# Decode cross scores head by head beneath the cross query panels, prompt head 0 with them, and four banks for the cross output tiles

## Chip, core and metric

The kernel runs on one core of one Trainium2 chip. The metric is the device time of one execution in microseconds. The engines are called PE (TensorE), DVE (VectorE), ACT (ScalarE), POOL (GpSimd) and SP (SyncE) as in the profile; each runs its own instructions in order and waits on semaphores.

## What is computed

One inference step of a one-layer decoder trunk for 256 prompt tokens and 8 decode users of one token each (264 token columns in all), width 2048. The part that matters here is the cross attention over 256 memory tokens, with 4 heads of 128:

```
def cross_attn(h, mk, mv, w_q, w_o):
    q = (h @ w_q).reshape(B, T, X_HEADS, X_HEAD_DIM)
    s = jnp.einsum('bthd,bmhd->bhtm', q, mk, preferred_element_type=jnp.float32) * (X_HEAD_DIM ** -0.5)
    p = jax.nn.softmax(s, axis=-1).astype(mv.dtype)
    o = jnp.einsum('bhtm,bmhd->bthd', p, mv).reshape(B, T, X_DIM)
    return o @ w_o
```

h is the normalised residual. All prompt tokens share one memory, whose keys and values the kernel computes itself (tile mkv). Each decode user b has its own cached memory keys and values. Before this stands the mixer with its output projection, behind it a SwiGLU of 5632 and a final norm. Everything is fp32.

## The kernel before

**Weight panels.** A projection is a list of panels of 2048x128 weights (1 MB). SP loads a panel into one of four raw slots. ACT rounds it to whi (L565, `cast`), DVE forms wlo = raw - whi (L993, `split`), and PE makes three matmuls for each of 16 blocks (L1554 to L1556, `three`): whi by hh, whi by hl, wlo by hh, all 264 columns wide, into one of banks 0 and 1. So a panel has 48 matmuls. DVE evicts the bank. The handshakes are the semaphores w_hi, w_split, mm_done and acc0_free / acc1_free. In `step`, ACT waits for the end of panel k before it casts panel k+2; DVE waits for the end of panel k, evicts its tile and then splits panel k+2. The order of the lists is: in, mem, out, xq, xo, gu0, dn0, gu1, dn1.

**xq** is the cross query projection: four panels, panel k giving head k of x_q (feature by token: 128 x 264; columns 256 to 263, called DEC, are the decode users). In its first panel PE also sums the squares of the norm (L1606, L1608); ACT takes the root (L579, with a table load), DVE the reciprocal (L1019), and `to_q` (L1385) multiplies each evicted tile by it.

**The block between xq and xo** has two interleaved parts, whose order is written out by hand on each engine.
Decode scores, user by user: DVE spreads x_q's column of user b on diagonals (`x_diag`, L1392, 128x512), PE multiplies it by ones so that every partition has the query of all four heads (`x_spread`, L1886, banks 2 and 3), ACT copies it scaled to x_qb (`x_query`, L858), and DVE makes eight products with sum (`x_scores`, L1401): two halves of the memory by four heads, keys in page (partition = memory token), each 128x128. The keys of all eight users have been loaded long before; the last product for user b releases POOL's fetch of the values of user b into the same page slot (`fetch`, L466). Then softmax over the memory for all 32 (user, head) pairs: maximum (L1453, transpose L1946, L1456, L1457, L1948), subtraction (L1462), Exp (L922), sums (L1467, L1952), reciprocal (L1469). `x_pv` (L1896) multiplies by the values per user, ACT takes the result (`x_take`, L864), `x_extract` (L1902) picks the diagonal.
Prompt heads 0 to 3: `x_stage` (ACT: a_q L869, a_v L870, a_vn L872), `x_head` (PE: transposes L1909, scores L1912), `x_max` (DVE: L1412 to L1414), `x_exp` (ACT, L878), `x_rec` (DVE), `x_scale` (ACT, L886), `x_turned` (PE, L1921), `x_pt` (ACT, L892), `x_out` (PE, L1928, L1929), `x_out_hi` (ACT, L896) and `x_out_lo` (DVE, L1423). Even heads use banks 6 and 7 and one set of buffers, odd heads banks 0 and 1 and another. In the block the order is heads 0 and 1 with the decode scores, then heads 2 and 3 with the rest.

**xo** is the cross output: four panels, each of which makes four output tiles of 12 matmuls (contraction over 4 heads), 16 tiles c = 4k + j in all, in banks 0 and 1 in turn. It starts when DVE has finished all of the block (xo_go). DVE adds each tile to the residual x_res (L1490), ACT makes the next norm's hh (`norm_hi`, L583) and the square (L591), which POOL adds up (L484), and DVE makes hl one tile later (`norm_lo`, L1014). The split of panel k+2 stands behind tile 3 of panel k. **gu0** follows, whose first panel waits block by block for hl and again contains the sum of squares.

## Time and profile before

| | us |
|---|---|
| median of 3 runs | 1657.13 (1654.46 to 1662.43) |
| the profiled execution, its own time | 1656.92 |
| its span | 1655.2 |
| PE busy, share | 1519.4, 92% |
| DVE, ACT, POOL busy | 1034.0, 617.6, 229.0 |
| mean granted clock of PE | 0.967 |

The span runs from the first to the last recorded instruction; what lies around it is the difference to the execution's own time. A granted clock of 1.0 is 2.4 GHz, of 0.5 it is 1.2 GHz; a value between them is a mean over a stretch. "Idle before" in a row is how long the engine stood still ahead of the instruction, and the name behind it is what ended that.

### The profile page before, as it was taken

How to read it: one execution, taken by the hardware profiler on the slowest of the kernel's cores; microseconds unless marked ns; L12 is line 12 of the kernel's file. 1: busy time of each engine (PE TensorE's matmuls, PEld its weight loads, DVE VectorE, ACT ScalarE, POOL GpSimd, SP SyncE). 2: the span in 40 equal slices, each digit the busy share in tenths (PEclk: the TensorE clock that was granted, in tenths of full speed). 3: DMA queues.
4: the chain of work that ended last, by engine and by line, in shares of the span. 5: the costliest groups of instructions: out<-in, count | busy, mean ns of one | idle time of the engine just before them, and what ended most of it. 6: DMA issues, size and time to landing. Idle time of an engine off the chain costs nothing.

```text
span 1655.2 us, 32624 instructions
## 1 busy us (share of the span) xinstructions
PE 1519.4 (92%) x12197; PEld 1399.3 (85%) x12197; DVE 1034.0 (62%) x3234; ACT 617.6 (37%) x725; POOL 229.0 (14%) x331
## 2 busy tenths in 40 slices
PE   4999987899998898996779999999999999999997
PEld 4999854577776677995579999999999999999996
DVE  4579899898977876656455555553445555554444
ACT  3343233232143553443344333333333333333443
POOL 3011222222222222330120000000000000000221
PEclk9999989899998999998789999999999999999998
DMA  8558999999998899453225555544555555553553
GB/s 318 178 186 304 402 365 404 404 372 375 379 387 295 294 377 402 167 179 120 77 102 178 177 180 184 185 163 146 185 175 204 180 180 184 186 182 123 183 182 122
DMA packets 78979, 388.42 MB, mean 235 GB/s; under 512 B 9096, under 2 KB 9872, under 8 KB 56864
## 3 DMA queue, kind: packets, MB, share of 16 engines
q1 hardware_dynamic: 35424, 230.90, 39.1%
q0 software_dynamic: 39376, 143.15, 23.1%
q10 hardware_dynamic: 4080, 13.12, 2.0%
q8 instruction: 53, 0.87, 0.2%
q14 instruction: 46, 0.38, 0.1%
HBM read 377.03 MB, written 10.10 MB: 234 GB/s over the span
## 4 chain that ended last, share of the span: by engine, by line
PE 75%; DVE 13%; DMA 5%; ACT 4%; issue 3%; POOLq 0%; ACTq 0%; DVEq 0%; SPq 0%; POOL 0%
PE bank L1554 23%; PE bank L1555 22%; PE bank L1556 22%; DVE page L1084 4%; DVE wlo L1028 2%; DMA page<-kc_dram 2%; PE bank L1711 2%; DMA page<-vc_dram 1%; DVE wlo L993 1%; ACT whi L602 1%; DMA raw<-p_out_dram 1%; ACT whi L565 1%; DMA raw<-p_in_dram 1%; DVE rstd L1019 1%; PE bank L1886 1%
## 5 line engine op out<-in xcount | busy, mean ns | idle before, releaser
L1554 PE MATMUL bank<-hh,whi 128*128 128x264 f32 (+1 forms) x2368 | 693.5, 293 | 36.2 <-DVE wlo L1028 23.5
L1555 PE MATMUL bank<-hl,whi 128*128 128x264 f32 (+1 forms) x2368 | 677.4, 286 | 0.0
L1556 PE MATMUL bank<-hh,wlo 128*128 128x264 f32 (+1 forms) x2368 | 677.1, 286 | 0.0
L993 DVE TENSOR_TENSOR wlo<-raw,whi 128x2048 fp32r<-128x2048 f32 (+1 forms) x174 | 356.2, 2047 | 281.4 <-ACT whi L565 281.4
L1554 PEld LDWEIGHTS bank<-hh,whi 128*128 128x128 f32 x2368 | 452.7, 191 | 72.9 <-issue 38.7
L565 ACT ACTIVATE whi<-raw 128x2048 fp32r<-128x2048 f32 (+1 forms) x174 | 299.3, 1720 | 545.0 <-PE bank L1556 537.6
L1555 PEld LDWEIGHTS bank<-hl,whi 128*128 128x128 f32 x2368 | 453.2, 191 | 0.5 <-issue 0.2
L1556 PEld LDWEIGHTS bank<-hh,wlo 128*128 128x128 f32 x2368 | 450.7, 190 | 0.0
L1084 DVE CUSTOM_DVE_ANT_0 page<-page,qb 128x128 f32<-128x128 f32 x1024 | 226.4, 284 | 18.3 <-ACT qb L647 11.3
L1554 PE MATMUL bank<-f_hi,whi 128*128 128x264 f32 x704 | 202.2, 287 | 7.5 <-DVE f_lo L1526 7.5
L1556 PE MATMUL bank<-f_hi,wlo 128*128 128x264 f32 x704 | 201.5, 286 | 0.0
L1555 PE MATMUL bank<-f_lo,whi 128*128 128x264 f32 x704 | 200.3, 285 | 0.0
L484 POOL TENSOR_TENSOR s_acc<-s_acc,s_sq 128x264 f32<-128x264 f32 x45 | 71.4, 1588 | 826.6 <-ACT s_sq L591 826.0
L602 ACT ACTIVATE whi<-raw 128x2048 fp32r<-128x2048 f32 x58 | 110.9, 1911 | 163.2 <-PE bank L1556 150.9
L1028 DVE TENSOR_TENSOR wlo<-raw,whi 128x2048 fp32r<-128x2048 f32 x58 | 138.1, 2380 | 40.9 <-ACT whi L602 40.8
L1554 PEld LDWEIGHTS bank<-f_hi,whi 128*128 128x128 f32 x704 | 134.0, 190 | 7.9 <-issue 7.9
L1555 PEld LDWEIGHTS bank<-f_lo,whi 128*128 128x128 f32 x704 | 134.2, 191 | 0.0
L1556 PEld LDWEIGHTS bank<-f_hi,wlo 128*128 128x128 f32 x704 | 134.0, 190 | 0.0
L466 POOL DMA_DIRECT2D page<-kc_dram x128 | 67.6, 529 | 323.0 <-DVE s_raw L1084 293.6
L1711 PE MATMUL bank<-page,prob 128*8 128x256 f32 x1024 | 80.6, 393 | 25.7 <-DMA page<-vc_dram 13.0
L466 POOL DMA_DIRECT2D page<-vc_dram x128 | 67.6, 528 | 147.7 <-PE bank L1711 89.5
L1084 DVE DVE_READ_ACCUMULATOR2_ANT s_raw<- 128x1 f32 x1024 | 82.1, 80 | 0.0
(295 smaller groups left out, 1441.9 us busy)
## 6 DMA issues: line engine op xcount, KB each, us to landing
raw<-p_gu_dram SPq DMA_DIRECT2D x88, 1024.0 KB, 4.9
page<-kc_dram POOLq DMA_DIRECT2D x128, 512.0 KB, 8.6
page<-vc_dram POOLq DMA_DIRECT2D x128, 512.0 KB, 9.1
raw<-p_in_dram SPq DMA_DIRECT2D x48, 1024.0 KB, 8.3
raw<-p_dn_dram SPq DMA_DIRECT2D x64, 704.0 KB, 4.1
raw<-p_out_dram SPq DMA_DIRECT2D x16, 1024.0 KB, 5.5
raw<-p_mem_dram SPq DMA_DIRECT2D x8, 1024.0 KB, 8.3
x_res<-x_fm_dram SPq DMA_DIRECT2D x8, 528.0 KB, 10.3
```

The costliest lines, as they stand in the source:

```text
L466: pool.dma_start(dst, src).then_inc(S(f"page_in{slot}"), 16)
L484: pch.link(pool.tensor_tensor(s_acc[:, :], s_acc[:, :], s_sq[:, c % 2, :], ALU.add))
L565: act.activation(whi[:, kk % 2, 0:blocks * P], raw[:, kk, 0:blocks * P], ACT.Copy).then_inc(S("w_hi"), 1)
L602: act.activation(whi[:, p % 2, :], raw[:, ring(p) % 4, :], ACT.Copy).then_inc(S("w_hi"), 1)
L993: tt(wlo[:, (k + 2) % 4, 0:blocks * P], raw[:, (k + 2) % 4, 0:blocks * P], whi[:, k % 2, 0:blocks * P], ALU.subtract).then_inc(S("w_split" ...
L1019: ch.link(dve.reciprocal(rstd[:, 0:n], rstd[:, 0:n]))
L1028: tt(wlo[:, k, :], raw[:, k, :], whi[:, p % 2, :], ALU.subtract).then_inc(S("w_split"), 1)
L1084: ins = dve.tensor_tensor_reduce(out=pk, in0=pk, in1=qb[:, P * h:P * h + P], scale=1.0, scalar=0.0, op0=ALU.mult, op1=ALU.add, accum_out=s ...
L1554: mm(out, blk(whi, k % 2, b), rh, start=start, stop=False)
L1555: mm(out, blk(whi, k % 2, b), rl, start=False, stop=False)
L1556: return mm(out, blk(wlo, k, b), rh, start=False, stop=stop)
L1711: last = mm(bank[4][32 * g:32 * g + H, 0:256], prob[:, u % 2, v, :], page[:, slot, 256 * g:256 * g + 256], start=v == 0, stop=v == PAGES - 1)
```

## The change

- The decode scores go head by head. When head h of x_q is there, PE transposes its eight decode columns to rows (`x_rows`, 8x128, bank 5), ACT copies them scaled to x_qr, and PE spreads each user's row over the partitions with a matmul of contraction 8 (one column of the identity, broadcast), eight of them, 128 columns each, into banks 2 and 3. DVE's products read the query straight from these banks. x_qd and x_qb are gone.
- PE's four xq panels are cut into quarters of four blocks. Between them stand, for panel k, the rows and the spread of head k-1; and prompt head 0: `x_head(0)` in panel 1, `x_turned` in panel 2, `x_out` in panel 3. ACT and DVE get the same order. So three heads of scores and prompt head 0 lie beneath the xq panels, the fourth head of scores and prompt heads 1 to 3 behind them.
- The fetch of a user's values is released by the score of the last head.
- xo's tile j of each panel goes to bank j, so that four tiles can be open. ACT casts the next panel ahead of norm_hi of tile 3, and DVE splits it after tile 0 of the next panel.
- Five semaphores of the softmax become two counted ones.

The diff, with the indentation cut by up to twelve blanks:

```diff
@@ -314,8 +314,7 @@
 x_q = view(at("x_q", C0 + 32 * TW, [P, XH, T]), XH, T)
-x_qd = at("x_qd", C0 + 4 * TW, [P, 512])
-x_qb = view(at("x_qb", C0 + 6 * TW, [P, 2, 512]), 2, 512)
+x_qr = at("x_qr", C0 + 4 * TW, [ND, XH * P])
 x_s = view(at("x_s", C0 + 10 * TW, [P, ND, 2, XH]), ND, 2, XH)
@@ -847,15 +846,10 @@
         step("out", i, k, C)
-step("xq", 0, 0, C)
-norm_root(2, T)
-for k in range(1, 4):
-    step("xq", 0, k, C)
-def x_query(b):
-    act.wait_ge(S("xq_ps"), b + 1)
-    if b >= 2:
-        act.wait_ge(S("xk_used"), b - 1)
-    act.activation(x_qb[:, b % 2, :], bank[2 + b % 2][:, :], ACT.Copy, scale=SCALE).then_inc(S("xq_b"), 1)
+def x_rows(k):
+    act.wait_ge(S("xq_ps"), k + 1)
+    act.activation(x_qr[:, P * k:P * k + P], bank[5][0:ND, 256:384], ACT.Copy, scale=SCALE).then_inc(S("xq_rows"), 1)
@@ -866,6 +860,7 @@
     wait_apart(act, "a_free", i + 1)
+    act.wait_ge(S(f"acc{i % 2}_free"), ACC["xq"] // 2 + i // 2 + 2)
     act.activation(a_q[:, :], x_q[:, i, 0:NP_], ACT.Copy, scale=SCALE)
@@ -895,52 +890,55 @@
+step("xq", 0, 0, C)
+norm_root(2, T)
+x_rows(0)
 x_stage(0)
+step("xq", 0, 1, C)
+x_exp(H)
+x_rows(1)
+x_scale(H)
+step("xq", 0, 2, C)
+x_pt(H)
+x_rows(2)
+step("xq", 0, 3, C)
+x_out_hi(H, 0)
+x_rows(3)
 x_stage(1)
-x_query(0)
-x_query(1)
-x_exp(H)
+x_stage(2)
 x_exp(H + 1)
-x_query(2)
-x_query(3)
-x_scale(H)
+x_exp(H + 2)
 x_scale(H + 1)
-x_pt(H)
 x_pt(H + 1)
-x_query(4)
-x_query(5)
-x_out_hi(H, 0)
-x_query(6)
-x_query(7)
-x_out_hi(H + 1, 1)
-x_stage(2)
-x_stage(3)
-x_exp(H + 2)
-x_exp(H + 3)
+x_scale(H + 2)
 act.wait_ge(S("x_sub"), 1)
 act.activation(x_p[:, :, :, 0:XH], x_s, ACT.Exp).then_inc(S("x_exp"), 1)
-x_scale(H + 2)
-x_scale(H + 3)
 x_pt(H + 2)
-x_pt(H + 3)
+x_out_hi(H + 1, 1)
 x_take(0)
+x_stage(3)
+x_exp(H + 3)
 x_take(1)
...
 x_take(2)
+x_scale(H + 3)
 x_take(3)
+x_pt(H + 3)
+x_take(4)
+x_take(5)
 x_out_hi(H + 3, 3)
-for b in range(4, ND):
-    x_take(b)
+x_take(6)
+x_take(7)
 act.wait_ge(S("xod_ready"), 1)
...
         c = 4 * k + j
+        if j == 3:
+            step("xo", 0, k, C)
         act.wait_ge(S(f"acc{j % 2}_free"), ACC["xo"] // 2 + c // 2 + 2)
...
         square(3, c, x_res[:, c:c + 1, :])
-    step("xo", 0, k, C)
@@ -1383,24 +1381,20 @@
     tt(x_q[:, k, :], bank[k % 2][:, 0:T], rstd[:, :], ALU.mult).then_inc(S(f"acc{k % 2}_free"), 1)
-panels("xq", to_q)
-ch.link(dve.memset(x_p, 0.0))
-def x_diag(b):
-    if b:
-        dve.wait_ge(S("xq_ps"), b)
-    tt(x_qd[:, :].rearrange("p (a b) -> p a b", a=XH), row(ident).broadcast_to([P, XH, P]),
-       x_q[:, :, NP_ + b:NP_ + b + 1].broadcast_to([P, XH, P]), ALU.mult).then_inc(S("xq_diag"), 1)
-def x_scores(b):
-    dve.wait_ge(S("xq_b"), b + 1)
-    dve.wait_ge(S(f"page_in{b}"), 16 * 33)
-    for m in range(2):
-        for h in range(XH):
+def x_scores(h):
+    dve.wait_ge(S("xq_spread"), h + 1)
+    for b in range(ND):
+        if h == 0:
+            dve.wait_ge(S(f"page_in{b}"), 16 * 33)
+        for m in range(2):
             pk = page[:, b, 512 * m + P * h:512 * m + P * h + P]
-            ins = dve.tensor_tensor_reduce(out=pk, in0=pk, in1=x_qb[:, b % 2, P * h:P * h + P], scale=1.0, scalar=0.0,
-                                           op0=ALU.mult, op1=ALU.add, accum_out=x_s[:, b, m, h:h + 1])
-    ins.then_inc(S("xk_used"), 1)
+            ins = dve.tensor_tensor_reduce(out=pk, in0=pk, in1=bank[2 + b // 4][:, P * (b % 4):P * (b % 4) + P], scale=1.0,
+                                           scalar=0.0, op0=ALU.mult, op1=ALU.add, accum_out=x_s[:, b, m, h:h + 1])
+        if h == XH - 1:
+            ins.then_inc(S("xk_used"), 1)
+    if h < XH - 1:
+        ins.then_inc(S("x_scored"), 1)
@@ -1424,50 +1418,43 @@
 x_start()
-x_diag(0)
+ch.link(dve.memset(x_p, 0.0))
+step("xq", 0, 0, C, to_q)
+x_scores(0)
 x_max(H)
-x_diag(1)
+step("xq", 0, 1, C, to_q)
+x_rec(H)
+x_scores(1)
+step("xq", 0, 2, C, to_q)
+x_scores(2)
+step("xq", 0, 3, C, to_q)
+x_out_lo(H, 0)
+x_start()
 x_max(H + 1)
-x_scores(0)
-x_diag(2)
-x_scores(1)
-x_diag(3)
-x_rec(H)
-x_rec(H + 1)
-x_scores(2)
-x_diag(4)
 x_scores(3)
-x_diag(5)
-x_scores(4)
-x_diag(6)
-x_scores(5)
-x_diag(7)
-x_out_lo(H, 0)
-x_scores(6)
-x_scores(7)
-x_out_lo(H + 1, 1)
-x_start()
-x_start()
 own("xk_used", ND)
 bh = "p (b h) -> p b h"
-tt(x_sm[:, 0:32].rearrange(bh, b=ND), x_s[:, :, 0, :], x_s[:, :, 1, :], ALU.max).then_inc(S("xmx_ready"), 1)
+tt(x_sm[:, 0:32].rearrange(bh, b=ND), x_s[:, :, 0, :], x_s[:, :, 1, :], ALU.max).then_inc(S("x_small"), 1)
+x_rec(H + 1)
 x_max(H + 2)
-dve.wait_ge(S("xmx_ps"), 1)
+dve.wait_ge(S("x_small_ps"), 1)
 ch.link(dve.tensor_reduce(x_sm[0:32, 64:65], bank[5][0:32, 0:P], AX.X, ALU.max))
-ts(x_sm[0:32, 96:128], ident[0:32, 0:32], x_sm[0:32, 64:65], None, ALU.mult).then_inc(S("xm_diag"), 1)
-x_max(H + 3)
-dve.wait_ge(S("xm_ps"), 1)
+ts(x_sm[0:32, 96:128], ident[0:32, 0:32], x_sm[0:32, 64:65], None, ALU.mult).then_inc(S("x_small"), 1)
+x_rec(H + 2)
+dve.wait_ge(S("x_small_ps"), 2)
 mb = bank[5][:, P:P + 32].rearrange(bh, b=ND)
...
 ins.then_inc(S("x_sub"), 1)
-x_rec(H + 2)
+dve.wait_ge(S("x_exp"), 1)
+tt(x_sm[:, 32:64].rearrange(bh, b=ND), x_p[:, :, 0, 0:XH], x_p[:, :, 1, 0:XH], ALU.add).then_inc(S("x_small"), 1)
+x_out_lo(H + 1, 1)
+x_start()
+dve.wait_ge(S("x_small_ps"), 3)
+dve.reciprocal(x_sm[:, 128:160], bank[5][:, 160:192]).then_inc(S("x_small"), 1)
+own("x_small", 4)
+x_max(H + 3)
 x_rec(H + 3)
-dve.wait_ge(S("x_exp"), 1)
-tt(x_sm[:, 32:64].rearrange(bh, b=ND), x_p[:, :, 0, 0:XH], x_p[:, :, 1, 0:XH], ALU.add).then_inc(S("xl_part"), 1)
-dve.wait_ge(S("xl_ps"), 1)
-dve.reciprocal(x_sm[:, 128:160], bank[5][:, 160:192]).then_inc(S("xl_read"), 1)
-own("xl_read", 1)
 x_out_lo(H + 2, 2)
@@ -1487,11 +1474,11 @@
         xs = x_res[:, c, :]
-        tt(xs, bank[j % 2][:, 0:T], xs, ALU.add).then_inc(S(f"acc{j % 2}_free"), 1)
+        tt(xs, bank[j][:, 0:T], xs, ALU.add).then_inc(S(f"acc{j % 2}_free"), 1)
         if c:
             norm_lo(3, c - 1, 3, x_res[:, c - 1, :], hh, hl, T)
-    if k < 3:
-        split(first, 0, k + 2, C)
+        if k and j == 0:
+            split(first, 0, k + 1, C)
 norm_lo(3, C - 1, 3, x_res[:, C - 1, :], hh, hl, T)
@@ -1877,13 +1864,36 @@
     out_panel(c)
-four_panels("xq")
-def x_spread(b):
-    pe.wait_ge(S("xq_diag"), b + 1)
-    if b >= 2:
-        pe.wait_ge(S("xq_b"), b - 1)
-    mm(bank[2 + b % 2][:, :], ones, x_qd[:, :], start=True, stop=True).then_inc(S("xq_ps"), 1)
+def x_quarter(k, q):
+    if q == 0:
+        pe.wait_ge(S("w_split"), ST["xq"][0] + k + 1)
+        pe.wait_ge(S(f"acc{k % 2}_free"), ACC["xq"] // 2 + k // 2 + 1)
+    for b in range(4 * q, 4 * q + 4):
+        if k == 0:
+            if b == C - 1:
+                norm_sum(2)
+            pe.wait_ge(S("n_lo_done"), 2 * C + b + 1)
+        last = three(bank[k % 2][:, 0:T], (k + 2) % 4, b, hh[:, b, 0:T], hl[:, b, 0:T], b == 0, b == C - 1)
+    if q == 3:
+        last.then_inc(S("mm_done"), 1)
+def x_rows(h):
+    pe.wait_ge(S(f"acc{h % 2}_free"), ACC["xq"] // 2 + h // 2 + 2)
+    if h:
+        pe.wait_ge(S("xq_rows"), h)
+    pe.transpose(bank[5][0:ND, 256:384], x_q[:, h, DEC], ident).then_inc(S("xq_ps"), 1)
+def x_spread(h):
+    pe.wait_ge(S("xq_rows"), h + 1)
+    if h:
+        pe.wait_ge(S("x_scored"), h)
+    for b in range(ND):
+        last = mm(bank[2 + b // 4][:, P * (b % 4):P * (b % 4) + P], ident[0:ND, b:b + 1].broadcast_to([ND, P]),
+                  x_qr[:, P * h:P * h + P], start=True, stop=True)
+    last.then_inc(S("xq_spread"), 1)
@@ -1928,38 +1938,52 @@
-x_head(0)
+for k in range(4):
+    x_quarter(k, 0)
+    if k:
+        x_rows(k - 1)
+    x_quarter(k, 1)
+    if k:
+        x_spread(k - 1)
+    x_quarter(k, 2)
+    if k == 1:
+        x_head(0)
+    elif k == 2:
+        x_turned(H)
+    elif k == 3:
+        x_out(H)
+    x_quarter(k, 3)
+x_rows(3)
+for k in range(2):
+    pe.wait_ge(S(f"acc{k}_free"), ACC["xq"] // 2 + 3)
 x_head(1)
-for b in range(4):
-    x_spread(b)
-x_turned(H)
+x_spread(3)
+x_head(2)
+pe.wait_ge(S("x_small"), 1)
+pe.transpose(bank[5][0:32, 0:P], x_sm[:, 0:32], ident).then_inc(S("x_small_ps"), 1)
 x_turned(H + 1)
-x_spread(4)
-x_spread(5)
-x_out(H)
-x_spread(6)
-x_spread(7)
+pe.wait_ge(S("x_small"), 2)
+mm(bank[5][:, P:P + 32], ones[0:32, :], x_sm[0:32, 96:128], start=True, stop=True).then_inc(S("x_small_ps"), 1)
+x_turned(H + 2)
 x_out(H + 1)
-x_head(2)
+pe.wait_ge(S("x_small"), 3)
+mm(bank[5][:, 160:192], ones, x_sm[:, 32:64], start=True, stop=True).then_inc(S("x_small_ps"), 1)
+x_pv(0)
 x_head(3)
-pe.wait_ge(S("xmx_ready"), 1)
-pe.transpose(bank[5][0:32, 0:P], x_sm[:, 0:32], ident).then_inc(S("xmx_ps"), 1)
-pe.wait_ge(S("xm_diag"), 1)
-mm(bank[5][:, P:P + 32], ones[0:32, :], x_sm[0:32, 96:128], start=True, stop=True).then_inc(S("xm_ps"), 1)
-x_turned(H + 2)
-x_turned(H + 3)
-pe.wait_ge(S("xl_part"), 1)
-mm(bank[5][:, 160:192], ones, x_sm[:, 32:64], start=True, stop=True).then_inc(S("xl_ps"), 1)
-x_pv(0)
 x_pv(1)
 x_out(H + 2)
-pe.wait_ge(S("xl_read"), 1)
+pe.wait_ge(S("x_small"), 4)
 x_extract(0)
...
 x_pv(3)
+x_turned(H + 3)
+x_extract(2)
+x_pv(4)
+x_extract(3)
+x_pv(5)
 x_out(H + 3)
-for b in range(4, ND + 2):
+for b in range(6, ND + 2):
     x_extract(b - 2)
@@ -1967,9 +1991,9 @@
     for j in range(4):
-        pe.wait_ge(S(f"acc{j % 2}_free"), ACC["xo"] // 2 + 2 * k + j // 2 + 1)
+        pe.wait_ge(S(f"acc{j % 2}_free"), ACC["xo"] // 2 + 2 * k + j // 2)
         for b in range(XH):
-            last = three(bank[j % 2][:, 0:T], (k + 2) % 4, XH * j + b, oh[:, b, :], ol[:, b, :], b == 0, b == XH - 1)
+            last = three(bank[j][:, 0:T], (k + 2) % 4, XH * j + b, oh[:, b, :], ol[:, b, :], b == 0, b == XH - 1)
         last.then_inc(S("xo_tile" if j < 3 else "mm_done"), 1)
```

## Rows read from the trace of the kernel before

**Rows 1.** The page, parts 1 and 2: busy time; and GB/s moved in 40 slices
```profile
PE 1519.4 (92%) x12197; PEld 1399.3 (85%) x12197; DVE 1034.0 (62%) x3234; ACT 617.6 (37%) x725; POOL 229.0 (14%) x331
...
GB/s 318 178 186 304 402 365 404 404 372 375 379 387 295 294 377 402 167 179 120 77 102 178 177 180 184 185 163 146 185 175 204 180 180 184 186 182 123 183 182 122
```

**Rows 2.** Windows of core 0: us, PE, PEld, DVE, ACT, POOL busy, PEclk, DMA share, GB/s
```profile
742.60:764.30 21.70, 19.15 (x144) 18.80 (x143) 9.70 (x7) 7.51 (x5) 0.00 (x0) 0.92 0.43 146
764.30:776.00 11.70, 5.72 (x15) 3.84 (x14) 5.65 (x8) 4.21 (x8) 0.00 (x0) 0.71 0.26 90
776.00:801.10 25.10, 15.19 (x30) 6.70 (x30) 20.52 (x142) 11.46 (x26) 5.25 (x8) 0.73 0.40 130
801.10:823.90 22.80, 17.31 (x177) 13.37 (x177) 5.91 (x19) 10.34 (x32) 0.43 (x1) 0.78 0.12 43
...
830.50:868.00 37.50, 28.63 (x191) 27.87 (x190) 19.61 (x30) 17.73 (x30) 9.39 (x13) 0.86 0.32 113
sum 125.40, PE 92.59 PEld 77.17 DVE 64.32 ACT 53.75 POOL 17.44; mean PE 15.43 PEld 12.86 DVE 10.72 ACT 8.96 POOL 2.91
```

**Rows 3.** The timeline beneath the xq panels: start us, us, engine, line, what, idle before
```profile
742.61 1.92 ACT L565 ACTIVATE whi<-raw 128x2048 fp32r<-128x2048 f32 x1 [3.51 <-PE bank L1556]
...
748.26 0.43 DVE L1385 TENSOR_TENSOR x_q<-bank,rstd 128x264 f32<-128x264 f32 x1
748.43 1.91 ACT L565 ACTIVATE whi<-raw 128x2048 fp32r<-128x2048 f32 x1 [2.11 <-PE bank L1556]
...
750.95 0.44 PE L1554 MATMUL bank<-hh,whi 128*128 128x264 f32 x1 [2.55 <-DVE wlo L993]
...
753.17 0.42 PE L1555 MATMUL bank<-hl,whi 128*128 128x264 f32 x1
...
753.39 0.42 PE L1556 MATMUL bank<-hh,wlo 128*128 128x264 f32 x1
...
764.41 1.91 ACT L565 ACTIVATE whi<-raw 128x2048 fp32r<-128x2048 f32 x1 [3.89 <-PE bank L1556]
```

**Rows 4.** Groups of the block, 764.3 to 823.9 us: count, busy us, mean ns, idle before
```profile
L1401 DVE CUSTOM_DVE_ANT_0 page<-page,x_qb 128x128 f32<-128x128 f32 x64 | 14.1, 287 | 0.0
L1886 PE MATMUL bank<-x_qd,kst 128*128 128x512 f32 x16 | 12.4, 867 | 6.3 <-DVE x_qd L1392 6.3
...
L1392 DVE TENSOR_TENSOR x_qd<-kst,x_q 128x512 f32<-128x512 f32 x8 | 5.5, 690 | 6.1 <-PE bank L1886 5.9 <-DVE x_p L1387 0.2
L1401 DVE DVE_READ_ACCUMULATOR2_ANT x_s<- 128x1 f32 x64 | 5.3, 82 | 0.0
L858 ACT ACTIVATE x_qb<-bank 128x512 f32<-128x512 f32 x8 | 4.8, 594 | 12.1 <-PE bank L1886 12.1
```

**Rows 5.** The timeline within the block
```profile
778.33 1.28 ACT L878 ACT_TABLE_LOAD   x1
...
803.93 1.92 PE L1912 MATMUL bank<-mkv,a_q 128*128 128x256 f32 x4
...
810.19 1.97 PE L1921 MATMUL bank<-kst,a_s 128*128 128x128 f32 x8 [3.18 <-ACT a_s L886]
...
813.51 0.28 ACT L864 ACTIVATE x_o<-bank 128x128 f32<-128x128 f32 x1 [0.71 <-PE bank L1896]
```

**Rows 6.** A group of VectorE over the whole span: a 128x128 copy out of a bank
```profile
L1235 DVE COPY t_s<-bank 128x128 f32<-128x128 f32 x8 | 2.2, 275 | 0.0
```

**Rows 7.** The timeline of ScalarE and VectorE in the xo panels
```profile
826.15 0.52 ACT L583 ACTIVATE hh<-x_res,gains 128x264 fp32r<-128x264 f32 x1 [2.57 <-DVE x_res L1490]
...
831.22 1.90 ACT L565 ACTIVATE whi<-raw 128x2048 fp32r<-128x2048 f32 x1
...
833.15 2.29 DVE L993 TENSOR_TENSOR wlo<-raw,whi 128x2048 fp32r<-128x2048 f32 x1 [2.16 <-ACT whi L565]
835.36 0.42 DVE L1490 TENSOR_TENSOR x_res<-bank,x_res 128x264 f32<-128x264 f32 x1
```

**Rows 8.** The instructions that fetch decode values: ns min/median/max, first and last start
```profile
L466 POOL DMA_DIRECT2D page<-cmv_dram x8: 709/710/713, 780.1 to 800.8; - x8
```

## The prediction

> **What bounds it now.** The page comes first: TensorE (PE) is busy 92% of the span [rows 1], so a change pays only where PE stands still or runs at its low clock. The table of windows comes next, because the share hides the stages: in the 125.4 us from 742.6 to 868.0 PE is busy 92.6, and its granted clock is 0.71 to 0.78 in the three stretches that make up the cross attention block [rows 2]. Everything that the change touches lies there. Beneath the xq panels PE waits for VectorE's split of panel 2 [rows 3]. From 764.4 to 823.9, 59.5 us, no weight panel runs: that is the block. In the xo panels PE stops once per panel, because evictions stand behind a split on VectorE [rows 7]. The timeline gives the order within each stretch, the groups the prices.
>
> Durations are those of the profiled execution: 1656.92 us, 1.7 above its span and 0.2 under the median 1657.13. Less than 0.5% from the median (1648.8 to 1665.4) is what a measurement of this kernel can hardly tell from no change.
>
> **Prices.** A panel is 48 matmuls; panel 1 of xq ran from 742.6 to 748.4, 5.8 us, so 0.12 each; at the low clock starts are 0.22 apart [rows 3], so the low clock costs 0.10 a matmul. Cast 1.9, split 2.3, eviction 0.43, norm_hi 0.52 [rows 3, 7]. The 64 score instructions took 14.1 us, 0.22 each, with the accumulator read beneath the next one [rows 4]: one head, 16 of them, is 3.5 us.
>
> **Part A, the xq panels (742.6 to 764.4 before).** They now carry three heads of decode scores and prompt head 0.
> - PE runs quarter 0 of panel 1 (1.45 us, to 744.05) and then waits for the eviction of tile 0, since the row transpose reads x_q. That eviction ends at 748.7, after Sqrt and reciprocal [rows 3]. For 4.65 us three quarters of panel 1 stand behind it in PE's queue. Before, PE worked through this and idled 2.55 us afterwards [rows 3].
> - The mean clock of 0.92 over 21.7 us [rows 2] is 3.5 us at the low level, right after that idle time. I carry the fall over to the new stall: some 20 matmuls at 0.10, 2.1 us.
> - x_spread(h) is 8 fp32 products, K=8, 128 columns, two passes each: no row has that shape. Eight 128-column transposes took 1.97 us at the low clock [rows 5], 0.25 each. Above: 16 x 0.25 = 3.9 us. Below: half of it at full clock, 1.8. I take 1.8 beneath the panels, where PE is hot: three are 5.4.
> - Head 0's V transposes and scores 1.1, four transposes 0.45, output 0.85, each about half of its low-clock row [rows 5]: 2.4. Three row transposes of 0.2: 0.6.
> - ScalarE copies each row (0.28 [rows 5]) in its own order. Walked through: quarter 1 ends at 751.6, spread 753.9, quarter 2 755.3, head 0 756.5, panel 1 757.9. ScalarE then casts to 759.9 and does head 0's Exp with its 1.28 us table load [rows 5]; the copy for head 1 is ready at 762.7, PE arrives at 761.2: 1.5 us. In the other rounds the copy is there first. VectorE's scores(0) and maximum end at 759.0, so eviction 1 and split 3 stand behind them 1.1 us, which PE, in quarter 0 of panel 2 until 759.4, hardly feels; scores(1) and (2) end before their evictions are due.
> - Sum from 742.6: panels 17.4, stall 4.65, clock 2.1, spreads 5.4, head 2.4, rows 0.6, copy 1.5 = 34.0, to 776.6. **A = +12.2 us.**
>
> SP loads the same panels, one after each finished panel; panels are now 9 us apart, so the loads hide. The x_p memset moves beneath VectorE's wait for Sqrt.
>
> **Part B, the block (59.5 us before).** Gone are eight diagonals (5.5 us), eight spreads through ones (16 passes, 12.4 busy and 6.3 idle) and eight copies of 512 columns (4.8, with 12.1 idle before them) [rows 4]. They formed a ring: diagonal, spread, copy, eight scores. After the panels only the last head's scores are left. From 776.6: cast 1.9, head 0's output copy 0.4, row copy 0.3, staging of head 1 0.8, with hand-offs 3.5; head 1's V transposes and scores at the low clock 2.1 (1.92 for the four passes [rows 5]); spread(3) between 1.8 and 3.9, I take 2.6; 16 scores 3.5. That is 11.7: decode scores are done at 788.3, before at 801.1.
> The tail from there (maximum over keys, Exp, sums, values, extraction, two prompt heads) took 22.8 us [rows 2]. It now also holds the rest of head 1: transposes 0.9 and output 1.7 at the low clock, 25.4. xo starts at 813.7. **B = 37.1 - 59.5 = -22.4 us.**
> POOL's eight fetches of decode values went out one per user between 780.1 and 800.8 [rows 8]; now the last head releases all eight between about 785 and 788. At 0.71 us each on POOL the last issue is near 791.5; 4.2 MB at the 404 GB/s of the page's best slices [rows 1] take 10.4 us, so the last lands by about 802 and the first values product at 797, the last at 810, find theirs. I cost them at nothing; if that cover fails, 3 us.
>
> **The operand in PSUM.** The scores now take their second input from a bank. A 128x128 copy from a bank takes 275 ns, the score instruction from SBUF 287 [rows 6, 4]: no surcharge shows, and I take none. Bounds: nothing, to an exposed accumulator read of 0.08 on each, 1.3 us a head.
> The Trainium skill says the contrary (VectorE: DVE Perf Modes, The TRN2 errata): a fixed 120 cycles from PSUM against 58 from SBUF, and its Rules for kernel authors advise a copy to SBUF where many operations follow. An estimate from that page is 65 ns more each, 4.1 us over 64; with half of it on the path the sum would be 1638.
>
> **Part C, xo to the end of gu0's first panel (823.9 to 868.3, 44.4 us).** Before, VectorE made the split for panel k+2 right after tile 3 of panel k, with cast 831.2, split 833.2 to 835.4 and only then an eviction [rows 7], while two banks let PE go two tiles on: a period of 10.6 us for 5.8 of work. Now four banks carry PE across the border, the cast starts before norm_hi of tile 3, and the split follows tile 0 of the next panel. From xo's start T: PE ends panel 0 at T+5.8; cast to 7.8, norm_hi(3) and norm_lo(3) to 8.9, split to 11.2, before PE needs it at 11.6. Then ScalarE, with four norm_hi and squares a panel, falls behind: cast to 15.3, split 16.3 to 18.6, PE stalls 1.2; cast to 22.7, split to 26.0, PE, done at 24.4, stalls 1.6. gu0's first panel with its norm sum takes 6.7: T+32.7. For bursts on ScalarE and POOL I add 1: T+33.7. **C = -10.7 us.**
>
> **Sum:** 12.2 - 22.4 - 10.7 = -20.9; 1656.9 - 20.9 = 1636.0.
>
> **The rivals.**
> - **Small costs add up** (15%). Spreads at 3.9 (+2.1 three times, +1.3) and slower scores, 3 us of it on the path: +10.6, 1646.6. For it: K=8 products and copies of eight rows have no row. Against: the transposes' rows.
> - **xo keeps half its stalls** (10%), since norm_lo(c-1) waits for ScalarE, which now casts first: 2.4 us more in three panels, 1643.
> - **Slower: the low clock rules** (5%). Quarters now end in small products that wait on other engines, and 2.55 us of idle time were followed by the low clock [rows 3]. Place and price: xq panels 1 to 3 (144 matmuls) and xo with gu0's first panel (240) at 0.10 each, 38 us, less the 2 charged, plus 4 in the block: +40, 1676. It decides from 20.9 / 0.10, some 210 of those 384 matmuls. Against: beneath the panels and in xo I find no gap over 1.6 us but the one of 4.65.
> The Trainium skill knows such a case (TensorE: Matmul & The Clock Gate, A second HAM failure mode): a kernel that cycled through PSUM banks with short idle times had its clock alternate.
> - **More overlaps** (12%). Head 1 hides in the tail (-2.6), spread(3) at full clock (-0.8), no fall in panel 1 (-2.1), xo without its lag (-2.5): 1628.
> - **The change buys nothing** (3%). Scores 1 and 2 hold the evictions and PE waits each time: what leaves the block stands in the panels. Each hold would need 10 us; a head's scores are 3.5.
>
> **How the numbers follow.** Forecast 55%, its own range 1630 to 1642. With the rivals next to it 1627 to 1650 holds 8 in 10. Faster by over 0.5%: forecast, more overlap, xo's rival and most of the small costs, less what I overlooked: 0.82. Within 0.5%: 0.12. Slower: 0.06.
>
> **What would show it.** A: the last xq panel ends near 776.6, PE waits once for 4.7 us on x_q, and head 0's Exp stands beneath the panels. B: the last decode score is near 788, xo's first matmul near 813.7, and no values product waits for a transfer. C: gu0's first panel ends 33.7 us after xo's start, with PE waits of under 3 us in it. Score instructions stay at 0.22 us. I am wrong if the xq panels end after 782, if the clock from 742 to 868 is under 0.8, or if xo's period stays over 8 us.

## The result, and the profile after

The median went from 1659.94 us (1654.46 to 1663.26, 7 runs) to 1648.53 us (1647.55 to 1649.99, 7 runs): ratio 0.9934, 95% interval 0.9919 to 0.9949. That is 11.4 us less; forecast were 20.9. The profiled execution took 1649.72 us with a span of 1648.0, 1.2 over its median, and the one of the kernel before lies 3.0 under its median. So this pair of traces (1656.92 and 1649.72) differs by 7.2 us only, and the stretches below are held against those 7.2.

Three stretches can be cut at the same marks in every trace: the xq panels after the first, the block, and xo with gu0's first panel. The marks are ScalarE's casts at the ends of xq's first and last panel and of gu0's first, and xo's first product.

| us | before | forecast | after | after less forecast |
|---|---|---|---|---|
| xq panel 0 to panel 3 | 21.8 | 34.0 | 43.6 | +9.6 |
| block | 59.5 | 37.1 | 36.1 | -1.0 |
| xo to the end of gu0's first panel | 44.5 | 33.7 | 38.35 | +4.65 |

The table of windows of the kernel after, first the three gaps between xq's panel ends, then block and tail, then xo (us, then PE, PEld, DVE, ACT, POOL busy, PEclk, DMA share, GB/s):

```profile
743.10:762.90 19.80, 15.05 (x74) 14.01 (x73) 9.42 (x39) 4.96 (x8) 0.00 (x0) 0.66 0.15 53
762.90:776.10 13.20, 11.65 (x71) 11.19 (x70) 6.29 (x35) 5.33 (x9) 0.00 (x0) 0.74 0.23 81
776.10:786.70 10.60, 10.60 (x70) 9.75 (x68) 6.14 (x34) 2.54 (x3) 0.00 (x0) 0.84 0.28 100
786.70:799.30 12.60, 8.68 (x30) 6.56 (x29) 7.96 (x38) 5.41 (x13) 2.55 (x4) 0.59 0.32 104
799.30:822.90 23.60, 16.20 (x180) 12.30 (x180) 6.72 (x23) 10.64 (x33) 3.20 (x6) 0.79 0.45 168
822.90:830.50 7.60, 7.60 (x50) 7.60 (x51) 2.24 (x5) 2.49 (x6) 1.86 (x4) 0.78 0.01 2
830.50:861.20 30.70, 26.30 (x198) 25.64 (x198) 22.29 (x31) 17.34 (x30) 16.27 (x14) 0.94 0.41 137
```

The clock beneath xq's panels was 0.92 [rows 2]; now it is 0.66, 0.74, 0.84. The last xq panel has no wait at all (10.60 busy of 10.60) and still takes 10.6 us, where the prediction's prices give 8.65 (5.8 for the panel, 1.8 for the spread, 0.85 for head 0's output, 0.2 for the row). TensorE's timeline beneath these panels shows the waits and the spreads:

```profile
749.31 0.38 PE L1886 MATMUL bank<-kst,x_q 128*8 128x128 f32 x1 [4.75 <-DVE x_q L1383]
752.25 3.78 PE L1894 MATMUL bank<-x_qr,kst 8*128 8x128 f32 x16
767.41 2.87 PE L1894 MATMUL bank<-x_qr,kst 8*128 8x128 f32 x16 [1.55 <-ACT x_qr L852]
779.06 2.04 PE L1894 MATMUL bank<-x_qr,kst 8*128 8x128 f32 x16
782.00 0.34 PE L1542 MATMUL bank<-hl,whi 128*128 128x264 f32 x1
782.13 0.42 PE L1543 MATMUL bank<-hh,wlo 128*128 128x264 f32 x1
782.36 0.42 PE L1541 MATMUL bank<-hh,whi 128*128 128x264 f32 x1
```

Both waits are the forecast ones, 4.75 for 4.65 and 1.55 for 1.5. But the clock falls three times, not once. It is at 0.50 from about 748 to 761.6, a fall that comes within the wait of 4.75 us and ahead of the first spread; from 768.5 to 775.3, a fall within the second spread, behind the wait of 1.55; and from 782.1 to 785.5. The last rows show this third one: inside panel matmuls, with nothing idle before them, 1 us after a spread, the starts go from 0.13 to 0.23 us apart. Of 135 recorded panel matmuls of the three panels, some 51 start 0.22 us after the one before, the others 0.12 after it.

The groups of the score instructions and of POOL's fetches, from 742 to 800 us, and the whole fetch on POOL's timeline:

```profile
L1392 DVE CUSTOM_DVE_ANT_0 page<-page,bank 128x128 f32<-128x128 f32 x64 | 13.6, 282 | 10.4 <-PE bank L1894 10.4
L1392 DVE DVE_READ_ACCUMULATOR2_ANT x_s<- 128x1 f32 x64 | 5.2, 82 | 0.0
...
796.75 5.74 POOL L465 DMA_DIRECT2D page<-cmv_dram  x8 [61.23 <-DVE x_s L1392]
```

A score instruction takes 282 ns from PSUM where it took 287 from SBUF [rows 4]. The fetches go out in one run at the end, from 796.75 to 802.5, and no values product waits for a transfer: the first starts at 808.76, where the forecast had 797.

The timeline of xo, one period of it:

```profile
830.52 1.92 ACT L564 ACTIVATE whi<-raw 128x2048 fp32r<-128x2048 f32 x1
833.24 0.77 POOL L483 TENSOR_TENSOR s_acc<-s_acc,s_sq 128x264 f32<-128x264 f32 x1 [2.03 <-ACT s_sq L590]
833.29 2.86 DVE L991 TENSOR_TENSOR wlo<-raw,whi 128x2048 fp32r<-128x2048 f32 x1
834.18 2.58 POOL L483 TENSOR_TENSOR s_acc<-s_acc,s_sq 128x264 f32<-128x264 f32 x1 [0.18 <-POOL s_acc L483]
838.17 1.90 ACT L564 ACTIVATE whi<-raw 128x2048 fp32r<-128x2048 f32 x1
...
843.82 0.39 PE L1541 MATMUL bank<-oh,whi 128*128 128x264 f32 x1 [1.55 <-DVE wlo L991]
852.72 0.36 PE L1541 MATMUL bank<-hh,whi 128*128 128x264 f32 x1 [2.85 <-issue]
```

The cast before, one panel after the one at 831.22 [rows 7]:

```profile
841.80 1.90 ACT L565 ACTIVATE whi<-raw 128x2048 fp32r<-128x2048 f32 x1
```

The period is 7.65 us (cast to cast), where it was 10.6, and my walk had 7.5. Two things are new. The split takes 2.86 us where it took 2.3 [rows 7]: it starts 0.05 us after a GpSimd addition of 0.77 us, and the next addition, which starts inside the split, takes 2.58 instead of 0.75 and ends 0.6 us behind it. And PE waits 2.85 us before gu0's first panel, 1.4 us beyond the end of the split that it needs (851.31).

### The profile page after: what moved, and what is told of

The parts are those of the page before. It is cut to its first block, busy times and chain, and to the rows that moved or that the text cites. A ratio compares the mean times of both kernels' runs of the same rounds, so it can differ in the third digit from the quotient of the medians.

```text
span 1648.0 us, 32704 instructions
## 1 busy us (share of the span) xinstructions
PE 1521.5 (92%) x12249; PEld 1408.8 (85%) x12249; DVE 1031.0 (63%) x3226; ACT 612.7 (37%) x721; POOL 235.1 (14%) x331
## 4 chain that ended last, share of the span: by engine, by line
PE 74%; DVE 14%; DMA 5%; ACT 4%; issue 3%; ACTq 0%; DVEq 0%; SPq 0%; POOLq 0%; POOL 0%
PE bank L1541 22%; PE bank L1542 21%; PE bank L1543 21%; DVE page L1082 4%; DVE wlo L1026 3%; DMA page<-kc_dram 2%; PE bank L1698 2%; ACT whi L601 1%; ACT whi L564 1%; DMA raw<-p_out_dram 1%; DVE wlo L991 1%; PE bank L1894 1%; DMA raw<-p_in_dram 1%; DMA page<-vc_dram 1%; DVE rstd L1017 1%
## 5 line engine op out<-in xcount | busy, mean ns | idle before, releaser
L1082 DVE CUSTOM_DVE_ANT_0 page<-page,qb 128x128 f32<-128x128 f32 x1024 | 226.2, 283 | 16.5 <-ACT qb L646 11.4
L483 POOL TENSOR_TENSOR s_acc<-s_acc,s_sq 128x264 f32<-128x264 f32 x45 | 77.5, 1723 | 815.5 <-ACT s_sq L590 814.4
L1698 PE MATMUL bank<-page,prob 128*8 128x256 f32 x1024 | 79.8, 389 | 24.1 <-issue 12.6
```

The lines of the kernel that those rows point to most:

```text
L483: pch.link(pool.tensor_tensor(s_acc[:, :], s_acc[:, :], s_sq[:, c % 2, :], ALU.add))
L1082: ins = dve.tensor_tensor_reduce(out=pk, in0=pk, in1=qb[:, P * h:P * h + P], scale=1.0, scalar=0.0, op0=ALU.mult, op1=ALU.add, accum_out=s ...
L1698: last = mm(bank[4][32 * g:32 * g + H, 0:256], prob[:, u % 2, v, :], page[:, slot, 256 * g:256 * g + 256], start=v == 0, stop=v == PAGES - 1)
```

## Experiments

Theory A: the fp32 products that contract over 8 rows take the clock down. Its rivals: the idle times do it, or the quarters' small pieces. For xo, D: a wait for a bank that is already free; and E: VectorE and GpSimd hold each other up.

**Spreads contracted over 128 rows** (kernel after; x_qr has 120 more rows of zeros, so that the products give the same):

```diff
-x_qr = at("x_qr", C0 + 4 * TW, [ND, XH * P])
+x_qr = at("x_qr", C0 + 4 * TW, [P, XH * P])
...
-last = mm(bank[2 + b // 4][...], ident[0:ND, b:b + 1].broadcast_to([ND, P]),
+last = mm(bank[2 + b // 4][...], ident[:, b:b + 1].broadcast_to([P, P]),
...
+ch.link(dve.memset(x_qr[:, :], 0.0))
```

> The changed kernel with one edit: the spread's products contract over 128 partitions instead of 8 (the rows of x_qr below the eighth are zero), same number of passes, same columns, same result. Theory A (the K=8 products themselves bring the low clock): in the changed kernel the clock is low from 748 to 761.6, 768.9 to 775.3 and 782.5 to 785.2, each around a spread; with K=128 the clock beneath the xq panels returns within 4 us of the 4.75 us stall and does not fall after the spreads of panels 2 and 3. The three xq panels after the first shorten from 43.6 to about 35 us, the time falls by 8 to 10 us, to about 1639. Theory B (only PE's waits bring it: 4.75 us on x_q, 1.55 us on the row copy): nothing changes beyond 1 us, the clock pattern stays, 1648.

1641.22 us (1638.44 to 1643.08), ratio to before 0.9882 (0.9863 to 0.9902), 7.3 us under the kernel after. Its windows from the end of xq panel 0 to that of panel 3:

```profile
746.80:762.90 16.10, 11.35 (x73) 11.03 (x72) 8.40 (x37) 4.94 (x7) 0.00 (x0) 0.79 0.17 65
762.90:772.90 10.00, 8.54 (x72) 8.19 (x71) 7.06 (x38) 5.35 (x9) 0.00 (x0) 1.00 0.30 107
772.90:781.50 8.60, 8.55 (x69) 8.21 (x67) 6.16 (x37) 2.56 (x4) 0.00 (x0) 1.00 0.36 123
```

43.6 us have become 34.7. The idle times and the pieces are all still there (4.75 and 1.46 us of waits), and from 759 us on the clock stays at 1.0 to the end of the panels. Only the fall at the long wait is left, the one that the prediction charged. So the rivals fall for the second and the third fall, and idle time stays the likely cause of the first.

One trace is not enough to price this. The spreads over 8 rows stand unchanged in four other kernels below. The one without xo's part again takes 43.6 us here; the other three take 37.7 to 37.9. All five show the three falls; what differs is the first, which lasts some 13.6 us in two of them and 3.4 in three. The windows of one of the three (the kernel of "Earlier cast and split in xo"):

```profile
748.00:763.70 15.70, 10.94 (x74) 10.27 (x73) 8.64 (x37) 4.98 (x8) 0.00 (x0) 0.89 0.19 67
763.70:775.40 11.70, 10.14 (x71) 9.79 (x70) 6.90 (x38) 5.33 (x10) 0.00 (x0) 0.85 0.27 91
775.40:786.00 10.60, 10.53 (x69) 9.65 (x67) 6.17 (x35) 2.57 (x4) 0.00 (x0) 0.84 0.28 100
```

Against those, the wider contraction takes off 3.8 us in the second and third gap (22.3 to 18.55) and nothing in the first (16.1). The medians are 7.3 us apart, and the runs of the two kernels don't overlap.

**The products by themselves**, in the kernel before, in the dense panels of the mixer's output projection: first one group each of 8 products over 8 and over 128 rows, behind the eighth block of panels 4 and 10, then longer groups in panels 2, 5, 9 and 13.

```diff
+if n == 7 and c in (2, 5, 9, 13):
+    kp, count = {2: (ND, 8), 5: (ND, 16), 9: (ND, 32), 13: (P, 32)}[c]
+    for d in range(count):
+        mm(bank[5][:, P * (d % 4):P * (d % 4) + P], ident[0:kp, d % 8:d % 8 + 1].broadcast_to([kp, P]),
+           x_res[0:kp, 0, 0:P], start=True, stop=True)
```

> The kernel before, with two groups of eight fp32 products of 128 columns (16 passes each, as one spread) put into the middle of two out panels, where PE never waits: contraction 8 in panel 4, contraction 128 in panel 10, same moving operand, into bank 5, where nobody reads them. Nothing of the computation is left out. Theory A: after the K=8 group the matmul starts go from 0.12 to 0.22 us apart for some us, without any idle time before; after the K=128 group they stay 0.12. Theory B: both stay at 0.12 and each group costs its own 1.8 us only.

> The kernel before, with groups of fp32 products of 128 columns inside out panels, where PE never waits, into bank 5, unread; nothing is left out. Panel 2: 8 products of contraction 8 (1.8 us, as one spread); panel 5: 16 (3.6 us); panel 9: 32 (7.1 us); panel 13: 32 of contraction 128. One group of 8 in dense work had left the clock at 1.0. Theory A2 (products of contraction 8 count as rest, so the clock falls when there are enough of them, or when other rest stands beside them): the clock falls in or after the 32 of panel 9, perhaps after the 16 of panel 5, and not after the 32 full ones of panel 13. Theory B (contraction does not matter): it stays 1.0 in all four.

The first (1664.15 us, one execution) did not show the effect: the clock stayed at 1.0 behind both groups. The second (1688.74 us, one execution) shows it, and more of it with more products. Its windows: three around the 16 products over 8 rows, which run from 678.1 to 683.1; three around the 32 over 8 rows, from 708.4 to 719.9; and one at the end of the 32 over 128 rows, which run from 745.4 to 752.7:

```profile
679.00:681.00 2.00, 2.00 (x18) 2.00 (x17) 1.48 (x2) 0.00 (x0) 1.19 (x1) 0.88 0.45 176
683.00:685.00 2.00, 2.00 (x9) 1.89 (x9) 0.00 (x0) 0.00 (x0) 0.00 (x0) 0.50 0.00 0
687.00:689.00 2.00, 2.00 (x17) 2.00 (x17) 0.43 (x1) 0.78 (x1) 0.00 (x0) 0.91 0.00 0
710.00:712.00 2.00, 2.00 (x17) 2.00 (x16) 0.76 (x1) 0.00 (x0) 0.47 (x1) 0.81 0.07 25
718.00:720.00 2.00, 2.00 (x10) 1.77 (x10) 0.00 (x0) 0.00 (x0) 0.00 (x0) 0.50 0.00 0
724.00:726.00 2.00, 2.00 (x15) 2.00 (x15) 0.43 (x1) 0.69 (x1) 0.00 (x0) 0.77 0.00 0
752.00:754.00 2.00, 2.00 (x19) 2.00 (x18) 0.00 (x0) 0.00 (x0) 0.00 (x0) 1.00 0.00 0
```

PE is busy 2.00 of 2.00 us in each, so no idle time comes in. 8 products over 8 rows: no fall. 16: low from 680.5 to 687.3. 32: low from 711.2 to 724.9. 32 over 128 rows: none. Both falls come while the products are still running. So these products themselves bring the low clock when there are enough of them. In the kernel after, a spread is only 8 products, and the clock falls within the second and behind the third, where one group of 8 in dense work did nothing; what else counts there (the wait of 1.55 us, row transposes, the falls before, the head's pieces) stays open.

**The two halves of the change alone.** xo's part in the kernel before, and the kernel after without it:

```diff
+if j == 3:
+    step("xo", 0, k, C)
-tt(xs, bank[j % 2][:, 0:T], xs, ALU.add)
+tt(xs, bank[j][:, 0:T], xs, ALU.add)
-if k < 3:
-    split(first, 0, k + 2, C)
+if k and j == 0:
+    split(first, 0, k + 1, C)
```

> The kernel before with the xo part alone (four banks, cast ahead of norm_hi of tile 3, split after tile 0 of the next panel). If the profile's split of the gain is right, xo to the end of gu0's first panel goes from 44.4 to 38 us and the time falls by 5 to 7 us (ratio about 0.996). Rival, my blind forecast: 33.7 us in that stretch and 10.7 us less, which would hold if the loss to 38.3 in the changed kernel comes only from the low clock at xo's start.

> The changed kernel without its xo part (two banks, old order of cast and split there). Sum of the stretches of the two profiles: xq panels +21.8, block -23.4, so about -1 to -2 us against before: the head by head order by itself is worth almost nothing (ratio 0.999). Rival: it is worth its forecast of -10 and the loss is in xo; then the ratio is 0.994.

xo's part alone: 1650.3 us (1649.78 to 1652.77), ratio 0.9948 (0.9932 to 0.9964), 9.8 under the kernel before as measured beside it (1660.11), more than the 5 to 7 expected. The rest alone: 1656.1 (1650.67 to 1667.79), ratio 0.9978 (0.9961 to 0.9994), 4.0 under. So most of the gain is xo's part: four banks, the earlier cast and the later split, which were not taken apart. The head-by-head scores, a restructured block, bring 4 us: what the block gives (36.2 in this trace for 59.5) the xq panels take (43.6 for 21.8), and xo's stretch grows from 44.5 to 45.9. The three stretches of this trace, of the second slowest of twelve executions (1659.82), add up to 125.7 us as before to 125.8, so the 4 us of the medians stand in none of them. xo's stretch is 36.8 us with xo's part alone, 38.35 in the kernel after; the difference is its start, where the clock is 1.0 in the one and 0.50 from 824 to 826 us in the other.

**A later order.** With spreads over 128 rows, PE transposes head 0's row two quarters later, behind quarter 2 of panel 1, and the spreads stand at the ends of the panels. Prompt head 0's scores move to panel 2, its four transposes to panel 3 and its output behind the panels. VectorE evicts a tile before it makes the scores of the head before, and the splits for xo's first two panels stand behind scores. ACT gets the same order. PE's part of the edit:

```diff
 for k in range(4):
     x_quarter(k, 0)
-    if k:
+    if k >= 2:
         x_rows(k - 1)
+    if k == 2:
+        x_head(0)
     x_quarter(k, 1)
...
     x_quarter(k, 2)
+    if k == 1:
+        x_rows(0)
     x_quarter(k, 3)
+    if k:
+        x_spread(k - 1)
```

> The changed kernel with contraction 128 in the spreads and a later order beneath the xq panels: PE does three quarters of panel 1 before it waits for x_q of head 0, a head's spread comes after the panel's last quarter, VectorE evicts a tile before the scores of the head before it, and the splits for xo's first two panels, which nobody is waiting for, stand behind scores. Theory: PE's 4.75 us stall shrinks to under 2 and the 1.55 us wait for the row copy goes; the three xq panels take 26 instead of 34.7 us, and the time is 8 us below that of the version with contraction 128 alone, about 1633. Rival: VectorE's scores, one head after each panel, become what PE waits for (before spread(2), spread(3)), and the block grows by what the panels lose: 1640.

1633.68 us (1630.56 to 1639.95), ratio 0.9839 (0.9815 to 0.9863): 7.5 under the kernel with spreads over 128 rows alone. Windows for xq and the block, and the one wait left beneath the panels:

```profile
750.40:775.30 24.90, 23.06 (x192) 22.70 (x191) 18.04 (x76) 12.85 (x19) 0.00 (x0) 1.00 0.37 127
775.30:813.00 37.70, 25.09 (x228) 19.04 (x227) 17.78 (x91) 16.17 (x46) 5.75 (x8) 0.77 0.38 140
...
756.62 0.27 PE L1889 MATMUL bank<-kst,x_q 128*8 128x128 f32 x1 [1.84 <-DVE x_q L1383]
```

xq takes 24.9 us, 3.1 more than before the change, with the clock at 1.00. Only two heads of decode scores lie beneath it now: the third spread ends behind the panels, and its 16 scores start at 777.1, behind the last eviction at 775.3. With head 0's output they are part of why the block takes 37.7 us for 34.7, so of the 9.8 us that xq gains the block gives 3 back.

**Earlier cast and split in xo** (kernel after):

```diff
-if j == 3:
+if j == 2:
     step("xo", 0, k, C)
...
+if k and j == 1:
+    split(first, 0, k + 1, C)
 if c:
     norm_lo(3, c - 1, 3, x_res[:, c - 1, :], hh, hl, T)
-if k and j == 0:
-    split(first, 0, k + 1, C)
```

> The changed kernel with xo's loop opened: ScalarE casts ahead of norm_hi of tile 2 instead of tile 3, VectorE evicts tile 1 of the next panel before the split instead of after it. Theory: the 7.6 us from cast to cast in xo are the serial loop cast, norm_hi, norm_lo, split, eviction, norm_hi; opened, it falls to about 6, PE's stalls of 1.55 and 2.85 us shrink to under 1 each, and xo with gu0's first panel goes from 38.4 to 34 us: 1644. Rival: PE is held by the split itself (stretched to 2.86 us while POOL adds), not by its place: 38, 1648.

1646.66 us (1645.96 to 1650.84), ratio 0.9926 (0.9906 to 0.9946). xo's stretch falls by 3.2 to 35.2 us (34 were expected), the casts stand 5.8, 6.9 and 6.3 apart, and PE's waits are 0.86 and 1.64 us for 1.55 and 2.85, where under 1 each was expected. The medians show 1.9 us, within the spread.

**The bank** (kernel after; gu0's first panels wait for one release less):

```diff
-pe.wait_ge(S(f"acc{k % 2}_free"), ACC[name] // 2 + 2 * i + k // 2 + 1)
+pe.wait_ge(S(f"acc{k % 2}_free"), ACC[name] // 2 + 2 * i + k // 2 + (0 if name == "gu0" and isinstance(i, int) and k < 2 else 1))
```

> The kernel after, with one edit: the first two panels of the first gate-and-up product wait for one release of the accumulator banks less, so that they start when their own bank is free and not when the fourth output tile is. Theory D (part of the 6.1 us that the cross output's stretch gained instead of the 10.7 forecast is a wait for a bank that is already free): TensorE's idle time before the second of these panels, 2.85 us in the kernel after, falls to about 1.5 us or under (the first panel's end is then set by the split values of output tile 14 alone), the stretch from the cross output's first product to the end of the first gate panel goes from 38.35 to about 37 us, and the time from 1648.5 to about 1647. Rival: the panel is held by its input (the split of the normalized rows) and not by the bank; then the idle time stays at 2.8 us and the stretch at 38.3.

1645.84 us (1636.78 to 1652.4), ratio 0.9929 (0.9908 to 0.9949): too wide to place 1.5 us. The trace does: its PE timeline and xo's window,

```profile
841.29 0.39 PE L1541 MATMUL bank<-hh,whi 128*128 128x264 f32 x1 [1.55 <-DVE wlo L991]
...
812.70:848.30 35.60, 32.42 (x244) 31.52 (x244) 24.50 (x36) 19.87 (x37) 18.12 (x17) 0.95 0.35 119
```

The 2.85 us put down to "issue" are 1.55 and now put down to the split, so 1.3 us were the count: gu0's first panel writes bank 0, and the count also held the eviction of tile 2 from bank 2. The stretch lost 2.8 us, not 1.3, and the clock no longer falls behind the shorter wait (0.50 at 854 to 856 us in the kernel after; here 1.00 from 818 us to the end of the stretch). The wait is that before the first gate panel, not the second as the expectation has it.

**GpSimd's additions left out** (kernel after; the sum of squares of the third norm is not made):

```diff
+if m != 3:
     pch.link(pool.tensor_tensor(s_acc[:, :], s_acc[:, :], s_sq[:, c % 2, :], ALU.add))
```

> The kernel after, with GpSimd's additions for the sum of squares of the third norm left out (so the FFN norm's scale is not the right one; that part of the computation is missing). Theory E (VectorE and GpSimd slow each other down when both stream rows at once): VectorE's second split step in the cross output, 2.86 us in the kernel after, goes back to the 2.29 us it took before, the distance between successive casts from 7.6 to about 7.0 us, the stretch from 38.35 to about 36.5, and the time from 1648.5 to about 1646.5. Rival: the longer split is a matter of what it reads and writes, not of its neighbour: it stays at 2.86 us, casts stay 7.6 us apart, and the time stays within 0.5 us of 1648.5.

1646.62 us (1645.65 to 1648.15), ratio 0.992 (0.9899 to 0.9941). The timeline has the split and the casts:

```profile
832.58 1.92 ACT L565 ACTIVATE whi<-raw 128x2048 fp32r<-128x2048 f32 x1
835.34 2.29 DVE L992 TENSOR_TENSOR wlo<-raw,whi 128x2048 fp32r<-128x2048 f32 x1
839.49 1.90 ACT L565 ACTIVATE whi<-raw 128x2048 fp32r<-128x2048 f32 x1
```

2.29 us instead of 2.86, the period 6.9 instead of 7.65, the stretch 34.6 us. Theory E holds: the longer split came from its neighbour. In the kernel after, the rows look like one engine standing until the other is done, not like both at a lower pace. All three long splits start within 0.06 us of an addition and take 0.57 longer; the additions that start inside them end 0.6 us behind them, which is little less than one takes alone. The medians (ratios 0.992 and 0.9934) can't tell this kernel from the kernel after. The stretch fell by 3.75 where 1.85 were expected: PE's waits in it are 0.46 and 1.94 us for 1.55 and 2.85, and no fall of the clock follows the second.

**All together.** The 128-row spreads, the later rows and the earlier cast and split; then these and the bank.

> Contraction 128, the later order and the opened xo loop together. If the three act on separate stretches: 1648.5 less 7.3, less 8, less 4.5, about 1629, ratio 0.981 to before. Rival: they share waits, and it stays above 1635.

> Spreads contracted over 128 rows, the later order of the row copies, the earlier cast and split in the cross output, and the bank wait of own_bank together. If the gains lie in different stretches they add: all three gave 1629.95 us, and own_bank's 1 to 1.5 us comes off it, 1628.5 us, with the cross output's stretch at about 34 us. If the earlier cast and split have already taken away the wait for the bank, the stretch stays at 35.2 and the time at 1630.

1629.95 us (1627.41 to 1634.13), ratio 0.9826 (0.9804 to 0.9849), and with the bank 1628.72 (1624.88 to 1635.25), ratio 0.9823 (0.9798 to 0.9847). Both are clear of both kernels; the bank's share can't be told in these medians, but xo's stretch is 33.9 us with it and 35.2 without. The windows of the last one, xq, block and xo:

```profile
744.40:769.30 24.90, 23.06 (x192) 22.70 (x191) 18.05 (x76) 12.85 (x19) 0.00 (x0) 1.00 0.36 127
769.30:805.50 36.20, 23.06 (x229) 17.89 (x227) 17.78 (x91) 16.17 (x46) 5.76 (x8) 0.86 0.41 146
805.50:839.40 33.90, 32.43 (x246) 31.68 (x247) 25.12 (x36) 19.98 (x37) 17.79 (x17) 0.95 0.36 125
```

## Why the prediction was right and wrong

The direction was right, and 1648.53 lies near the upper end of 1627 to 1650; the size was not right: 11 us instead of 21. Point by point:

- **Part A failed**, +21.8 instead of +12.2, and the failed terms are "clock 2.1" and "spreads 5.4". The waits came as walked. The spreads took 3.78 + 2.87 + 2.04 = 8.7 us, 3.3 over. The clock on the panels' own matmuls cost 51 of 135, or some 54 of 144 at 0.10, 5.4 us, 3.3 over. Head 0's pieces took 1.8 + 0.7 + 1.4 = 3.9 us for 2.4, since each fell in a low stretch. That is 8.1 of the 9.6 us; the rest lies in small joints. The failed step is the sentence "I take 1.8 beneath the panels, where PE is hot", with one fall of the clock charged: spreads over 8 rows brought two more falls, and over 128 rows they did not. The length of the first fall differs between executions of the same code, for a reason that no run shows: in three of the five profiles with this code the stretch took 37.8 us, 3.8 over the forecast instead of 9.6. The rival "the low clock rules" had the effect and named a cause for it, small products that wait on other engines; with the same waits and wider contractions the clock stayed up behind the second and third spread, so that cause falls too. Its price was 38 us, and some 8.5 came, 5.4 here and 3.1 in xo. The rival "small costs add up" came near in the number (1646.6) and mostly by luck: its spreads were dear (8.7 of its 11.7), its slower scores never came.
- **Part B held**: 36.1 us for 37.1. Decode scores ended 12.6 us after the panels (11.7), the tail took 23.6 (25.4). The cover for POOL's fetches held, with the last issue done at 802.5 and not near 791.5.
- **The operand in PSUM** costs nothing: 282 ns. By the 65 ns more that I estimated from the Trainium skill (VectorE: DVE Perf Modes, The TRN2 errata) it would have been some 350 ns; the trace disagrees for this instruction, and going against the page was right.
- **Part C was half right**: 38.35 us, not 33.7. The walk of casts and splits (a period of 7.5) came out at 7.65. Beyond it, at its start PE came out of the block at the low clock (0.78 in the first 7.6 us, some 1.6 us, which xo's part alone doesn't have). PE's waits were 1.55 and 2.85 us, 1.6 over the walk's 1.2 and 1.6, from the splits that GpSimd held up by 0.57 us each and from the bank's count, 1.3 us. The low clock behind the second wait cost about 1.5. The 1 us that I added for bursts should have been 5.6, of which these are 4.7; the rest is open. The rival "xo keeps half its stalls" said 2.4 us in three panels, with another cause.
- A's +9.6, B's -1.0 and C's +4.65 are 13.3 us in all, the medians show 9.5. This pair of traces lies 4.2 us closer than the medians (3.0 in the kernel before, 1.2 in the kernel after), and its start differs by 0.5.

The condition "I am wrong if the xq panels end after 782, if the clock from 742 to 868 is under 0.8" was met in its first half (786.7), and that is where most of the error was. The clock from 742 to 868 us was 0.80, at the edge of the second half; before it was 0.82.

## What to carry to other kernels

When a matmul with a very short contraction goes into dense TensorE work, price not only its own time but the low clock behind it, and try it padded with zero rows: that alone gave 7.3 us here. When small pieces are put between panels to hide work, ask of each piece which result it waits for: a later order, in which the first row transpose stood two quarters later, gave as much again. Count a wait by the bank it is for, not by a count that several banks share: here the trace showed such a wait as "issue". And where the clock has a part, look at several profiles of the same code before pricing it: 43.6 us in two and 37.8 in three were the same instructions.

## What the runs showed of the hardware

- In dense work, 16 fp32 products over 8 rows (128 columns, two passes each) brought 6.8 us at 0.50, beginning within them, and 32 brought 13.7 us; 8 brought none, nor did 32 over 128 rows (one execution each). The 64 passes over 8 rows took 11.47 us, low clock included.
- VectorE's subtraction of 128x2048 took 2.86 us when a GpSimd addition of 0.77 us had just started and 2.29 without it; an addition that started within it took 2.58 us instead of 0.75.
- A product with sum of 128x128 took 282 ns with its second input in PSUM, 287 with it in SBUF.
